# Routing bias loaded first, half of the token matrix waited for later, and a small expert's tokens gathered at its own beginning

## What is computed

```python
logits = (tok @ router_w).astype(jnp.float32) + router_b.astype(jnp.float32)
probs = jax.nn.softmax(logits, axis=-1)
top_p, top_i = lax.top_k(probs, TOP_K)
top_p = top_p / jnp.sum(top_p, axis=-1, keepdims=True)
...
for ex in range(N_EXPERTS):
    y = y + gate[:, ex:ex + 1].astype(tok.dtype) * swiglu(tok, w_gate_up[ex], w_down[ex])
...
h = h + rms_norm(ff, m_post_norm[j])
```

## Time and profile before

| | us |
|---|---|
| median of 3 runs | 1352.91 (1350.77 to 1357.46) |
| the profiled execution, its own time | 1353.34 |
| its span, first to last instruction | 1351.4 |
| PE busy | 1290.0 (95%) |
| DVE, ACT, POOL busy | 422.1, 347.6, 50.6 |
| PE in an expert's gate and up (L934) | 344.1 from `ring_low`, 149.8 from `ring_high` |
| read from device memory | 421.56 MB, 313 GB/s over the span |

### The profile page before, as it was taken

The page is one execution under the profiler, slowest core; times in us unless marked ns, Lnnn a source line. Parts: engine busy times, 40 slices in busy tenths (PEclk is TensorE's granted clock), DMA queues, the critical chain, the costliest instruction groups (busy, mean ns, idle before and its releaser), DMA issues.

```text
span 1351.4 us, 26213 instructions
## 1 busy us (share of the span) xinstructions
PE 1290.0 (95%) x11388; PEld 744.0 (55%) x11388; DVE 422.1 (31%) x807; ACT 347.6 (26%) x660; POOL 50.6 (4%) x77
## 2 busy tenths in 40 slices
PE   8989999999889989999999999999999989999986
PEld 7988999999788873443343443333443332343331
DVE  7785866653697731001010001000001000000102
ACT  7886544443567630000000000000000000000001
POOL 3001100001120010000000000000000000000000
PEclk9999999999999979999999999999999999999999
DMA  9538455555223398999999999999999999999994
GB/s 288 166 97 265 127 186 183 162 185 161 69 96 110 116 376 320 356 366 397 417 418 418 416 417 419 416 418 419 415 417 419 416 418 419 416 418 418 417 418 186
DMA packets 128133, 424.34 MB, mean 314 GB/s; under 512 B 8321, under 2 KB 77185, under 8 KB 99345
## 3 DMA queue, kind: packets, MB, share of 16 engines
q1 hardware_dynamic: 127664, 421.58, 80.4%
q0 software_dynamic: 352, 1.06, 0.2%
HBM read 421.56 MB, written 1.05 MB: 313 GB/s over the span
## 4 chain that ended last, share of the span: by engine, by line
PE 70%; SPq 13%; DMA 7%; DVE 5%; ACT 3%; issue 2%; DVEq 0%; POOL 0%; ACTq 0%
PE bank L934 29%; SPq L1058 12%; PE bank L911 10%; PE bank L530 9%; PE bank L532 8%; PE bank L531 8%; DMA ring_low<-in_m_w_gate_up 4%; DMA ring_low<-in_m_w_down 2%; PE bank L889 1%; PE bank L870 1%; PE bank L901 1%; PE bank L903 1%; DMA rbias<-in_gain_rows 1%; DVE w_lo L1579 1%; ACT w_hi L1181 1%
## 5 line engine op out<-in xcount | busy, mean ns | idle before, releaser
L934 PE MATMUL bank<-ring_low,x_T 128*32 128x512 f32 (+1 forms) x3552 | 344.1, 541 | 9.4 <-DMA ring_low<-in_m_w_gate_up 8.1
L934 PEld LDWEIGHTS bank<-ring_low,x_T 128*32 128x32 f32 x3552 | 113.3, 110 | 234.3 <-issue 210.5
L911 PE MATMUL bank<-ring_low,eT 128*32 128x512 f32 x1632 | 182.4, 594 | 11.9 <-DMA ring_low<-in_m_w_down 11.9
L530 PE MATMUL bank<-u_hi,w_hi 128*128 128x272 f32 (+1 forms) x568 | 166.4, 293 | 7.0 <-DVE u_lo L1634 5.1
L1579 DVE TENSOR_TENSOR w_lo<-raw,w_hi 128x2048 fp32r<-128x2048 f32 (+7 forms) x89 | 143.9, 1638 | 93.6 <-ACT w_hi L1181 93.4
L532 PE MATMUL bank<-u_hi,w_lo 128*128 128x272 f32 (+1 forms) x568 | 164.2, 289 | 0.0
L531 PE MATMUL bank<-u_lo,w_hi 128*128 128x272 f32 (+1 forms) x568 | 163.5, 288 | 0.0
L2072 DVE TENSOR_TENSOR e_h<-bank,e_h 128x512 f32<-128x512 f32 (+1 forms) x40 | 22.7, 618 | 416.9 <-PE bank L934 416.9
L934 PE MATMUL bank<-ring_high,x_T 128*32 128x384 f32 (+1 forms) x1568 | 149.8, 536 | 0.0
L1181 ACT CAST w_hi<-raw 128x2048 fp32r<-128x2048 f32 (+7 forms) x89 | 117.9, 1352 | 52.9 <-PE bank L532 52.9
L911 PEld LDWEIGHTS bank<-ring_low,eT 128*32 128x32 f32 x1632 | 50.1, 110 | 135.1 <-issue 111.9
(11 more groups left out here) (321 smaller groups left out, 1353.0 us busy)
## 6 DMA issues: line engine op xcount, KB each, us to landing
ring_low<-in_m_w_gate_up SPq DMA_DIRECT2D x92, 1024.0 KB, 23.1
ring_low<-in_m_w_down SPq DMA_DIRECT2D x80, 1024.0 KB, 23.8
ring_low<-in_m_w_gate_up SPq DMA_DIRECT2D x88, 768.0 KB, 22.0
ring_high<-in_m_w_gate_up SPq DMA_DIRECT2D x36, 1024.0 KB, 24.5
ring_high<-in_m_w_down SPq DMA_DIRECT2D x32, 1024.0 KB, 24.7
ring_high<-in_m_w_gate_up SPq DMA_DIRECT2D x40, 768.0 KB, 21.8
raw<-in_f_w_gate_up SPq DMA_DIRECT2D x24, 1024.0 KB, 5.3
raw<-in_f_w_down SPq DMA_DIRECT2D x12, 1024.0 KB, 5.2
```

The lines of the kernel that those rows point to most:

```text
L530: nc.tensor.matmul(o, a[0], b[0], start=start, stop=False)
L911: return nc.tensor.matmul(strip(q, t, NT), eT[u][:, bank, P * i + GROUP * at:P * i + GROUP * at + GROUP], w[:, n, :], start=start, stop=stop)
L934: last = nc.tensor.matmul(strip(q + 3 * (kind_of == "up"), t, width), x_T[:, part, group(g)], w[:, width * n:width * n + width], start=(pa ...
```

## The change

1. `rbias` is declared before the large tiles, and its load is POOL's first instruction. DVE waits for it alone (`in_bias`); `grow` keeps its load and gets its own semaphore, which DVE waits for at the last norm.
2. PE waits at an expert's chunk 0 for ACT's half of `x_T` only, and for DVE's half at chunk 4.
3. The SMALL expert's tokens are gathered by PE right ahead of its own chunk 0, no longer in BIG's down stage. `sel` is written by DVE as early as before. ACT and DVE take these two halves after BIG's down stage, ahead of the copies of `y_big`. The next BIG expert's tokens are gathered in SMALL's down stage, as before.

```diff
         first = sb("first", [P, NB * NE])[:, :]
+        rbias = sb("rbias", [P, NE])
...
-        rbias = sb("rbias", [P, NE])
...
-                def gather_x(half):
-
-                    pe.wait_ge(sel_done, ex + 2)
+                def gather_x(half, own):
+
+                    pe.wait_ge(sel_done, ex + 2 - own)
...
-                    emark(last, ("x", half))
+                    emark(last, ("own_x" if own else "x", half))
...
+                if kind == SMALL:
+                    for half in range(2):
+                        gather_x(half, own=1)
                 for c, (kind_of, u, part) in enumerate(EPLAN):
...
                             pe.wait_ge(x_by_act, ex * 4 + 4)
-                            pe.wait_ge(x_by_dve, ex * 4 + 4)
                             if kind == BIG:
                                 pe.wait_ge(scatter_added, it * 4 + 4)
+                        if c == 4:
+                            pe.wait_ge(x_by_dve, ex * 4 + 4)
...
-                        for half in range(2):
-                            gather_x(half)
+                        if kind == SMALL:
+                            for half in range(2):
+                                gather_x(half, own=0)
                         turn_gated()
...
+            pool.dma_start(rbias[:], gain_rows[0:1, D:D + NE].to_broadcast([P, NE])).then_inc(in_bias, 16)
             pool.wait_ge(in_par, 16)
...
-            pool.dma_start(grow[:], gain_rows[0:1, 0:D].to_broadcast([P, D])).then_inc(in_rows, 16)
-            pool.dma_start(rbias[:], gain_rows[0:1, D:D + NE].to_broadcast([P, NE])).then_inc(in_rows, 16)
+            pool.dma_start(grow[:], gain_rows[0:1, 0:D].to_broadcast([P, D])).then_inc(in_grow, 16)
...
-                at_expert(act, it, kind, "x", 0)
+                if kind == BIG:
+                    at_expert(act, it, SMALL, "own_x", 0)
+                else:
+                    at_expert(act, it, SMALL, "x", 0)
                 take_x(banks[3])
...
-            dve.wait_ge(in_rows, 32)
+            dve.wait_ge(in_bias, 16)
...
-                at_expert(dve, it, kind, "x", 1)
-                take_x(banks[4])
+                if kind == SMALL:
+                    at_expert(dve, it, kind, "x", 1)
+                    take_x(banks[4])
...
+                if kind == BIG:
+                    at_expert(dve, it, SMALL, "own_x", 1)
+                    take_x(banks[4])
                 at_expert(dve, it, kind, "chunk", EC - 1)
...
+            dve.wait_ge(in_grow, 16)
```

More of the change, by code:

```diff
@@ L397, in yoco_kernel @@
         hi_done, lo_done = sem("hi_done"), sem("lo_done")
-        in_const, in_par, in_rows, in_ident = sem("in_const"), sem("in_par"), sem("in_rows"), sem("in_ident")
+        in_const, in_par, in_bias, in_grow, in_ident = (
+            sem("in_const"), sem("in_par"), sem("in_bias"), sem("in_grow"), sem("in_ident"))
         in_x = [sem(f"in_x{b}") for b in range(3)]
```

## The result

The changed kernel took 1337.33 us in the median of 4 runs (1335.67 to 1339.88), the kernel before beside it 1351.84 (4 runs). The ratio is 0.9889, with a 95% interval of 0.9852 to 0.9926: 14.5 us less. The profiled execution took 1335.90 us, its span, first to last instruction, is 1333.9 (before: 1353.34 and 1351.4).

The account below looks back on a forecast made before the run. Loads bound the second half, and PE's arrival at the first SMALL expert's chunk 4 sets its start. From 1353.34 us, 3.3 for the earlier first chunk and 1 for placement gave 1349.0, against the median 1348.6; range 1342.5 to 1353.0.

Parts of the forecast that it names:

- The bound: Experts' stage: end is PE finishing the first SMALL expert's chunk 4, plus bytes left at 417 GB/s, plus an unchanged tail.
- what moves without being meant: Loads from 640 to 1325 us: ring_low moves 32 bytes to a multiple of 256; 1 us better taken.
- Case (c): Long load stretch: loads into the shifted ring are 1% faster or more, giving 1344.5 us or less; chance 0.12.
- about 1337: Loads into ring_low: if the read rule on 256-byte starts held for writes, a further 12 us would go.
- Part 1, the bias: Routing: DVE's sum runs without waiting for rbias; the choice comes 2.75 us earlier, of which 2.06 arrive at the gather.
- The cost of the early load: Kernel start: the added rbias load lies under POOL's first wait; taken as 0, at most 0.5 us.
- Part 2, the later wait: First chunk: PE goes on at the gather's end without waiting for DVE's half of the copy; 1.2 us saved.
- Case (a): Routing's gather: clock stays up at 2.4 GHz, gain 5.4 us in place of 3.3, time 1346.5; chance 0.2.
- Rival (b): Experts' dense chunks: a 6.8 us stretch at 1.2 GHz reaches them, losing 3.4 us, time 1352; chance 0.12.
- Part 3, the gather: First BIG and SMALL pair: PE passes SMALL's chunk 4 at the same distance from the start; 0 us.
- (d): Last loads: the slow DMA engines' 11 us lag grows; doubled, the time is 1360 us; chance 0.05.
- (e): Routing: the change doesn't do what it says, since another wait holds DVE's sum; chance 0.01.

Follow-up runs that it names:

- e1: Kernel before plus only an unused 32-byte tile, putting ring_low on a multiple of 256; 1342.99 us, ratio 0.992.
- e10: Kernel before with 192 unused bytes ahead of ring_high, putting it alone on a multiple of 256; 1351.36 us, ratio 0.9972.
- e12: Changed kernel with 32 more unused bytes in front: ring_low 32 and ring_high 96 beyond a multiple of 256; 1349.34 us, ratio 0.9971.
- e2: Changed kernel with the tile small cut by 32 bytes, so ring_low is back at 24,800; 1354.38 us, ratio 0.9995.
- e3: Changed kernel with 192 unused bytes ahead of ring_high, so both rings begin on a multiple of 256; 1335.54 us, ratio 0.9858.
- e4: Kernel before with only the early rbias load and DVE's wait for it, ring_low at 24,800; 1354.47 us, ratio 0.9996.
- e13: e9 plus two more unread PE products between the turns of the new rows' two blocks; 1335.04 us, ratio 0.9865.
- e9: Changed kernel with rbias loaded some 36 us later and both rings on a multiple of 256; 1337.77 us, ratio 0.9882.
- e5: Kernel before with only PE's wait for DVE's half moved to chunk 4, ring_low at 24,800; 1354.17 us, ratio 0.9994.
- e8: Changed kernel with POOL's rbias load moved some 36 us later, behind its store of the gain row; 1337.26 us, ratio 0.9875.
- e7: Kernel before with only the SMALL expert's gather moved ahead of its own chunk 0, ring_low at 24,800; 1354.47 us, ratio 1.0003.

## Why the prediction was wrong, step by step

**The bound was right.** The loads set the second half, share 1.01 in both, and the end was PE's chunk 4 plus the bytes left plus the same tail (14.94 and 14.83).

**The step that failed** is the term "what moves without being meant". It named the cause, that `ring_low` would come to a multiple of 256, but took 1 us for it and bounded it by 1% of the 485 us of `ring_low`, 5 us. It measured 11.4 us: 0.8% of the whole time in e1, 2.0% for a load. The bound came from comparing windows with loads of `ring_high` (64 beyond) with one of `ring_low` (224 beyond). Both are off the multiple, and e10 to e12 show that all five distances tried, 32 to 224 bytes, cost the same. The trace of before held no load at a multiple of 256, so it could not bound this cost. That the three rates stood close together said only that two bad positions are alike. Case (c) was the right case; its chance of 0.12 and the range's end at 1342.5 rested on that same comparison.

The rule of the page "DMA: Bandwidth & Descriptors", section "How a descriptor splits into AXI transactions", in the Trainium skill, was discarded on the same rows. Its direction holds here for writes: a start at a multiple of 256 bytes is cheaper. Its proportion doesn't. Estimated by its beats, 32 beyond would cost 1 in 257 and 224 beyond 7 in 263, and e12's `ring_low` at 32 measured 2.490 us against 2.491 at 224. One further piece for each row of 8 KB, 33 in place of 32, would cost alike for all distances; that would be 3% and a load gained 2.0 to 2.2%, so this is only argued. The prediction's last sentence on the rule, "about 1337", stands beside the measured 1337.33, but not by its working. The 1.9% that it names is 9.2 us of 485; its 12 us come out only with 7 beats in 263 (12.9 us) less the 1 us already taken. And of the measured difference the loads themselves gave 9.7 us, the smaller lag 1.6, and the order in the profiled pair 6.8 where 3.3 were forecast. That the two figures meet is luck.

**Part 1, the bias.** Right in its path: the sum at 488.01 (forecast 488.2), L1960 behind PE's product at 493.26 (forecast 492.3), PE's L824 right behind the unread products, and 1.48 us from there to the gather (forecast 1.58). The gather came 13.98 us behind the first turn, before 16.24: 2.26 us of gain where 2.06 were forecast. The cost of the early load was taken at 0, at most 0.5 us. That was too low: in the five kernels that load `rbias` first (after, e2, e3, e4, e12) that ACT step starts at 7.58 to 7.95 us, in the others at 6.50 to 6.87, 1.1 us later. At the first turn three of them (after, e3, e12) stand at 483.7 to 483.9, the eight others without the load or the filler at 483.0 in the mean (482.5 to 483.7). e2 and e4 stand at 486.8 and 485.5, and e13, without the early load and with its filler only behind the first turn, at 486.0. These three alone had a granted clock of 0.50 in the first 30 us, while PE multiplied the first layer's first products: e2 from 14.7 to 21.5, e4 from 15.9 to 19.3, e13 from 14.5 to 17.9 (and from 96.4 to 103.2, where e9 has 94.3 to 97.7). Windows of e2 and of the changed kernel, columns as in the earlier trace rows:

```profile
14.70:21.50 6.80, 6.80 (x30) 6.36 (x30) 6.76 (x11) 6.77 (x9) 0.00 (x0) 0.50 1.13 336
```

```profile
14.70:21.50 6.80, 6.80 (x54) 6.54 (x53) 6.77 (x10) 6.56 (x9) 0.00 (x0) 1.00 1.10 385
```

PE was busy throughout in both, with 30 records in place of 54. e2 is 0.35 us behind the changed kernel where that stretch of work begins (15.78 against 15.43) and 2.9 us where it ends (30.52 against 27.61), and reaches the first turn 3.1 us behind it, e4 1.7. Half of 6.8 is 3.4, half of e4's 3.4 is 1.7. So it is the clock that costs e2 and e4 their further 2 to 3 us in the profiled executions. Whether it fell in their other executions too no trace shows, nor why it fell in these.

**Part 2, the later wait.** 1.2 us forecast, 1.27 gone in e5 and in the changed kernel. But the estimate of 4.8 us from the gather's start to the loop's entry was too long: after a gather of 3.78 us the first chunk followed 3.71 us behind its start, since PE's load of `rounds_i` began 1.9 us behind it (499.6) and not 3.1.

**The clock.** Case (a) came true in the profiled execution: the clock fell at 489.1, rose at 495.9, and stayed up, so the gather lasted 3.78 us. With no limit by the loop's entry it gave 2.26 + 3.18 + 1.27 = 6.7 us, the table's 6.8. The change doesn't ensure it: e8 and e4 ran it at 1.2 GHz, e2, e3, e9 and e12 at 2.4. By the spans above, three of the changed kernel's four executions were like the profiled one. Rival (b) didn't happen: the first chunks ran at full clock, as everything behind 495.9.

**Part 3, the gather.** 0 forecast, and 0 found: first chunk to chunk 4 took 129.54 us, before 129.23. The cover of the copies was 4.5 us where 4.4 were forecast, the gap at 590 closed, and a new one opened at 630. The one forecast at the new gather was shallow: the share was 1.01 from 613 to 617, and 0.82 and 0.86 in the windows from 617 to 625. e7 showed the price of what hides it, 1.18 us without part 2.

**The order together** was forecast at 3.3 us. It measured 0.7 us (-1.2 to 2.4) in e2 and 3.9 us (0.9 to 6.9) in e12, and the changed kernel's ratio stands 0.3% (4 us) below e1's with overlapping intervals. By the times it is worth somewhere between 0 and 4 us. The spans say more: 1.5 us in e2, 4.9 and 5.2 in the changed kernel and in e12, so about 5 us where the start and the gather mostly keep the clock, beside the 6.8 us of the profiled pair. How much of it the early load takes back isn't settled.

**The other rivals.** (d) fell: the lag of the slow engines was 10.97 us, not over 12.56. (e) fell: nothing else held DVE's sum. Forecast 3.3 + 1; measured some 1.5 to 5 in the spans for the one, 11.4 for the other.

## What to carry to other kernels

Compute the byte position of every tile that large loads write, before and after an edit, and put the ones of a load-bound stretch on a multiple of 256 bytes: a declaration of 32 bytes in front of them was worth more than all of the reordering. When two rows are compared to bound a cost, ask first whether one of them is free of it; two rows that both pay it bound nothing. A microsecond won in front of a load-bound stretch arrives, but here it is smaller than what one execution differs from the next by its clock (4 us) and by the time outside its span (3 us): compare spans as well as times, and look at the granted clock of each profile before comparing starts.

## What the runs showed of the hardware that I had not expected

- A load of 1 MB in rows of 8 KB a partition takes 2.49 us at 32, 64, 96, 128 or 224 bytes beyond a multiple of 256 and 2.43 to 2.44 us on one, when the other ring's loads are off it.
- With both rings on a multiple every load takes 2.453 us, that is 1,048,576 B / 2.453 us = 427 GB/s, and the average over a turn of the ring is no better than with `ring_low` alone. So something else limits the loads there; no run shows what.
- The 16 DMA engines don't keep step. The last part of a load lands about 2 us behind its first part at 650 us, and of the last load 12.5 to 13.0 us behind where neither ring is on the multiple, 10.2 to 11.1 us where `ring_low` is. The lag doesn't grow evenly: in the kernel before and in the changed one it stays nearly level and then rises by 1.2 to 1.7 us within a few loads, about once in 45 loads and six times in the long stretch. Why is not shown.
- A broadcast load of 128 rows of 32 bytes, issued as the first, goes with a first large ACT step, which waits for the tokens' landing, that starts 1.1 us later (five kernels against nine).
- The granted clock of the same instructions differs from kernel to kernel where nothing ahead of them does: 3.78 or 6.82 us for the same 32 records. In e13's profile it fell at 492.3 us although PE was busy without a pause for 6.8 us before.
